# Attention heads with half units in another place, outputs by groups of four heads, and a mixer in another order

## The reference

```python
y = concatenate([o_a, o_b])            # layer 0: 10 sparse heads, 6 dilated heads
x = x + (y * silu(gate)) @ w_out       # layer 1: 8 stick breaking heads, 8 forgetting heads

# the second block
x = x + 0.5 * rmsnorm(swiglu(rmsnorm(x)))            # width 5632
o = gb[0] * o_cmp + gb[1] * o_sel + gb[2] * o_win    # 8 heads, 2 groups of keys and values
h = rglru(conv(xb)) * gelu(yb)                       # 1024 channels, the recurrent part
x = x + rmsnorm(concatenate([rmsnorm(o), rmsnorm(h)]) @ w_out)
x = x + 0.5 * rmsnorm(swiglu(rmsnorm(x)))            # width 5632 again
x = x + rmsnorm((gelu(x @ w_ple_gate) ...) @ w_ple_proj)
```

## Time and profile before

| what | value |
|---|---|
| time, median of 3 runs | 3042.7 us (3040.08 to 3045.18) |
| the profiled execution: time, span | 3044.3 us, 3042.5 us |
| PE busy in the span | 2920.7 us, 96% |
| DVE busy | 1728.0 us, 57% |
| ACT busy | 1298.8 us, 43% |
| POOL busy | 14.2 us |
| DMA | 530.6 MB, 174 GB/s |
| chain of waits that ended last | PE 64%, DVE 4%, ACT 2% |
| layer 0's heads | 280 to 366 us |
| layer 1's last head | 871 us |
| mixer, first unit to w_out's first | 1744 to 2090 us |

### The profile page before, as it was taken

How to read it: one execution, slowest core, us unless ns; L and a number is a source line. 1 busy time by engine, 2 the same in 40 slices (tenths; PEclk the granted TensorE clock), 3 DMA queues, 4 the chain that set the end, 5 groups by cost and what they waited for, 6 DMA issues and landing times.

```text
span 3042.5 us, 33344 instructions
## 1 busy us (share of the span) xinstructions
PE 2920.7 (96%) x13590; PEld 2419.7 (80%) x13590; DVE 1728.0 (57%) x1622; ACT 1298.8 (43%) x1340; POOL 14.2 (0%) x17
## 2 busy tenths in 40 slices
PE   8999899999989999999999999777999999999997
PEld 7878788878878888888888788665788888888876
DVE  5468755445465555555555744764655555555574
ACT  5444444344444433333433545443443333333453
POOL 0000000000000000000000000000000000000000
PEclk9999999999999999999999999997999999999999
DMA  6545255544445555555555554412565555555544
GB/s 237 194 147 183 95 183 180 193 165 165 134 140 186 196 192 193 193 190 188 188 193 192 168 186 166 165 56 97 169 208 193 193 189 188 188 193 191 189 170 141
DMA packets 275615, 530.60 MB, mean 174 GB/s; under 512 B 8640, under 2 KB 30288, under 8 KB 274752
## 3 DMA queue, kind: packets, MB, share of 16 engines
q1 hardware_dynamic: 275088, 528.25, 51.8%
q0 software_dynamic: 432, 0.99, 0.1%
HBM read 527.12 MB, written 2.10 MB: 174 GB/s over the span
## 4 chain that ended last, share of the span: by engine, by line
PE 64%; DVE 4%; ACT 2%; issue 1%; DMA 0%; SPq 0%; DVEq 0%; ACTq 0%
PE ps L594 19%; PE ps L596 19%; PE ps L595 19%; PE ps L612 1%; PE ps L613 1%; PE ps L614 1%; PE ps L674 1%; DVE w_lo L1615 1%; PE ps L760 0%; ACT w_hi L1101 0%; PE ps L1058 0%; PE ps L704 0%; PE ps L780 0%; DVE st L1848 0%; DMA raw<-in_w_in 0%
## 5 line engine op out<-in xcount | busy, mean ns | idle before, releaser
L1615 DVE TENSOR_TENSOR w_lo<-raw,w_hi 128x2048 fp32r<-128x2048 f32 (+2 forms) x503 | 1126.8, 2244 | 833.2 <-ACT w_hi L1101 831.6
L1101 ACT ACTIVATE w_hi<-raw 128x2048 fp32r<-128x2048 f32 (+2 forms) x503 | 942.0, 1878 | 1028.0 <-DMA raw<-in_ff_w_down 320.5
L594 PE MATMUL ps<-w_hi,x_hi 128*128 128x512 f32 (+3 forms) x3176 | 1234.0, 389 | 11.9 <-DVE w_lo L1615 11.9
L596 PE MATMUL ps<-w_hi,x_lo 128*128 128x512 f32 (+3 forms) x3176 | 1225.0, 386 | 0.0
L595 PE MATMUL ps<-w_lo,x_hi 128*128 128x512 f32 (+3 forms) x3176 | 1224.3, 385 | 0.0
L594 PEld LDWEIGHTS ps<-w_hi,x_hi 128*128 128x128 f32 x3176 | 599.3, 189 | 133.6 <-DVE w_lo L1615 11.3
L596 PEld LDWEIGHTS ps<-w_hi,x_lo 128*128 128x128 f32 x3176 | 598.3, 188 | 119.3
L595 PEld LDWEIGHTS ps<-w_lo,x_hi 128*128 128x128 f32 x3176 | 599.3, 189 | 116.1
L594 PE MATMUL ps<-w_hi,h_hi 128*128 128x512 f32 x652 | 254.8, 391 | 2.0 <-DVE h_lo L2331 2.0
L595 PE MATMUL ps<-w_lo,h_hi 128*128 128x512 f32 x652 | 254.5, 390 | 0.0
L596 PE MATMUL ps<-w_hi,h_lo 128*128 128x512 f32 x652 | 254.3, 390 | 0.0
(11 more groups left out here) (290 smaller groups left out, 1542.3 us busy)
## 6 DMA issues: line engine op xcount, KB each, us to landing
raw<-in_w_in SPq DMA_DIRECT2D x143, 1024.0 KB, 5.0
raw<-in_ff_w_gate SPq DMA_DIRECT2D x88, 1024.0 KB, 5.0
raw<-in_ff_w_up SPq DMA_DIRECT2D x88, 1024.0 KB, 5.0
raw<-in_ff_w_down SPq DMA_DIRECT2D x88, 1024.0 KB, 5.1
raw<-in_w_out SPq DMA_DIRECT2D x48, 1024.0 KB, 5.0
raw<-in_w_ple_gate SPq DMA_DIRECT2D x16, 1024.0 KB, 5.1
z<-in_rows SPq DMA_DIRECT2D x5, 1024.0 KB, 7.2
raw<-in_w_in SPq DMA_DIRECT2D x8, 536.0 KB, 3.6
```

The lines of the kernel that those rows point to most:

```text
L594: nc.tensor.matmul(o, x[0][:, k0 + c, s], hi[:, c, 0:width], start=first and c == 0, stop=False)
L596: m = nc.tensor.matmul(o, x[1][:, k0 + c, s], hi[:, c, 0:width], start=False, stop=last and c == n - 1)
L1101: nc.scalar.activation(landed_part(w_hi, u, j), landed_part(raw, u, j), ACT.Copy).then_inc(hi_ready, 1)
L1615: V.tensor_tensor(landed_part(w_lo, u, j), landed_part(raw, u, j), landed_part(w_hi, u, j).bitcast(F32), ALU.subtract).then_inc(parts_read ...
```

## The change

**Layer 0's heads.** On PE the half unit of an iteration moves behind `logits(n+1)`. ACT and DVE keep their orders.

**Outputs by four heads, layers 0 and 1.** The plan interleaves the first two column blocks of w_out unit by unit, so that both take the units of group 0 first, then of group 1, and so on. `gate_heads(layer, g)` for groups 0 and 1 stands in DVE's loop of heads (behind heads 9 and 13, and behind 28 and 30), for 2 and 3 behind it. PE transposes group 0 in front of `mix` of head 10 in layer 0, and between units at head 30 in layer 1, where the first unit of w_out runs beside head 31.

**The mixer.** The compressed part's columns come first, then a block of 352, then five blocks interleaved: 348 columns, `w1` of the keys, 348 columns, `w1` of the values, 512 columns. Queries, window and selected keys follow. Each kind's four heads of a group follow one another: four window, four selected, four window, four selected. The second block of queries and 7 halves and more of w_out (the recurrent part's rows first) run as half units behind `logits(n+1)` of a head. The compressed part becomes two transposes of a padded tile and four 128x512 matmuls, and one addition for four heads. `out_gain` has a buffer of its own; the block with `out_part` is kept in SBUF and added later. The norm of the attention part is summed by groups. SP loads in the new order, with the small weights behind the keys' `w1`; POOL's clearing of the buffer is gone.

```diff
-    L0_OUT = plan(t["w_out0"], 0, [BW] * 4)
+    L0_OUT = out_blocks(t["w_out0"])
...
+    def out_blocks(w):
+        k = [(c, UC) for c in range(0, KC, UC)]
+        first = in_turn([(w, 0, BW, k), (w, BW, BW, k)], [0, 1] * 4)
+        plan(w, 2 * BW, [BW] * 2)
+        return first
...
-    MIX_REC = plan(t["w_in_2"], ZG, [BW] * 3 + [268, 268])
-    MIX_QKV = plan(t["w_in_2"], 0, [BW] * 5)
-    CMP = plan_other(4)
+    MIX_COMPRESSED = plan(t["w_in_2"], ZKC, [BW])
+    MIX_REC = plan(t["w_in_2"], ZG, [352])
+    MIX_TOGETHER = in_turn([...],
+                           [0, 0, 1, 0, 1, 0, 1, 2, 1, 2, 2, 3, 2, 3, 4, 3, 4, 3, 4, 4])
...
+    halves_beside = [2, 2, 1, 1, 1, 1, 0, 0] + [1] * 7 + [0]
...
                         turn_qk(n + 1)
-                    if n < 16:
-                        advance_half(n % 2)
-                    if n > n0:
+                    if n == 46:
+                        turn_compressed()
+                    elif n == 11:
+                        turn_y(0, 0)
+                    if n > n0 and (n < 16 or n >= 32):
                         mix(n - 1)
-                    if n >= 16:
+                    if 16 < n < 32:
+                        mix(n - 1)
+                    if n == 30:
+                        advance(1)
+                        turn_y(1, 0)
+                        advance(2)
+                    elif n == 31:
+                        next_y(1)
+                    elif 16 <= n < 32:
                         advance(beside[n])
                     if n + 1 < n1:
                         logits(n + 1)
+                    if n < 16:
+                        advance_half(n % 2)
+                    elif n >= 32:
+                        advance_halves(n)
+                    if n >= 46:
+                        mix_compressed(n - 46)
                     turn_probs(n)
+                if n1 == 48:
+                    advance_half(1)
+                    mix(47)
+                    return
+                layer = n1 // 16 - 1
+                turn_y(layer, 1)
+                next_y(layer)
                 mix(n1 - 1)
+                next_y(layer)
+                turn_y(layer, 2)
+                next_y(layer)
+                turn_y(layer, 3)
+                while at[0] < first_unit[OUT_OF[layer] + 2]:
+                    next_y(layer)
...
+            def mix_compressed(g):
+                bank = 2 * pair_of[OUT_PART]
+                if g == 0:
+                    pe.wait_ge(made["cmp_p_copied"], 1)
+                else:
+                    pe.wait_ge(made["cmp_added"], g)
+                for tt in range(NT):
+                    i = nc.tensor.matmul(ps[:, bank + tt, :], cmp_pT[:, tt * P:(tt + 1) * P],
+                                         cmp_vs[:, g * BW:(g + 1) * BW], start=True, stop=True)
...
+                    if n in (9, 28):
+                        gate_heads(n // 16, 0)
+                    elif n in (13, 30):
+                        gate_heads(n // 16, 1)
```

More of the change, by code:

```diff
@@ L481, in _ @@
                 load_block(L0_GATE + b)
-            for b in range(4):
-                load_block(L0_OUT + b)
+            load_units(first_unit[L0_OUT], end_unit[L0_OUT + 3])
             sp.wait_ge(group_gated, 4)
@@ L989, in _ @@
                 i.then_inc(made[done], 1)
-                advance(2)
-            advance(4)
-            pe.wait_ge(made["rec_out_squared"], 1)
-            for b in range(LB):
-                i = nc.tensor.matmul(ps[:, 4, 0:SEQ], ones[:], by_block(r2)[:, b, :], start=b == 0, stop=b == LB - 1)
-            i.then_inc(made["rec_summed"], 1)
-            advance(2)
+            until(first_unit[MIX_TOGETHER])
+            pe.wait_ge(st_done, turned_before["mix"] + 8)
             pe.wait_ge(rotated, 3)
-            pe.wait_ge(made["rec_norm_root"], 1)
             for m, c0 in enumerate((ZKC, ZVC)):
@@ L1040, in _ @@
-            i.then_inc(made["cmp_kv_made"], 1)
-            pe.wait_ge(made["cmp_kv_ready"], 1)
+            for k in range(2):
+                i = nc.tensor.matmul(ps[:, 7, P:2 * P], cmp_hidT_heads[:, k, :], cmp_w2[:, 1, k, :],
+                                     start=k == 0, stop=k == 1)
+            i.then_inc(made["cmp_kv_made"], 1)
+            until(first_unit[MIX_SELECTED] + 1)
+            pe.wait_ge(made["rec_out_squared"], 1)
+            for b in range(LB):
+                i = nc.tensor.matmul(ps[:, 4, 0:SEQ], ones[:], by_block(r2)[:, b, :], start=b == 0, stop=b == LB - 1)
@@ L1067, in _ @@
+            for s in range(4):
+                turn_attention(s)
+                if s == 1:
+                    pe.wait_ge(st_done, turned_before["attn"] + 2)
+                    advance(1)
+            pe.wait_ge(st_done, turned_before["attn"] + 4)
+            until(end_unit[MIX_OUT + 3] - 1)
             advance_by_tile(signal=True)
@@ L1138, in drain @@
                     i.then_inc(drained[pair_of[b]], 1)
+                elif kind == "part":
+                    for tt in range(NT):
+                        i = nc.scalar.activation(out_part[:, tt], summed(b)[:, tt], ACT.Copy)
+                    i.then_inc(drained[pair_of[b]], 1)
+                elif kind == "output" and b == MIX_OUT + 2:
+                    act.wait_ge(made["part_added"], 1)
+                    tail_sums([out_part[:, tt] for tt in range(NT)], 2)
                 elif kind == "output":
@@ new lines, in _ @@
+            advance(1)
+            for tt in range(NT):
+                if tt == 0:
+                    act.wait_ge(made["attn_left"], 1)
+                else:
+                    act.wait_ge(out_written, 48)
+                attention_squares(tt, 1, made["attn_squared"])
+                act.wait_ge(made["attn_squared"], 3 + tt)
+                if tt == 0:
+                    act.wait_ge(made["attn_based"], 1)
+                nc.scalar.activation(attn_root[:, tt:tt + 1], attn_ssq[:, tt, 1:2], ACT.Sqrt,
+                                     bias=attn_base[:, tt:tt + 1]).then_inc(made["attn_rooted"], 1)
```

754 lines of the change are left out of this document (476 added, 278 removed).

## The result

The changed kernel took 3023.3 us in the median of 4 runs (3023.0 to 3024.7), the kernel before 3041.8 us in the same session (4 runs, 3040.1 to 3045.2). The ratio is 0.9939 with a 95% interval of 0.9921 to 0.9956. A second session gave 3027.3 us (3023.9 to 3029.4) against 3040.9, ratio 0.9951 (0.9933 to 0.9967). So the change saves 13.5 to 18.5 us, where 34.5 were forecast. The sign held, and both medians lie in the whole range of 2983 to 3032; the second lies outside the 2990 to 3025 that went with the likeliest course. The size was 39 to 54% of the forecast.

What follows compares the result with a forecast made beforehand. PE, busy 96% of the 3042.5 us span, was taken as the bound. Terms +11.5 - 9 - 42 + 5 = -34.5 against 3044.3 gave 3009.8, less 1.6: 3008 us; likeliest range 2990 to 3025, whole range 2983 to 3032.

Steps and rivals of the forecast that it cites:

- Part 1: Layer 0's heads: half unit behind the next logits makes a pair 12.5 us instead of 10.06; 7.5 pairs cost 18.4.
- The walk: Row-by-row timing of the changed heads in layer 0 and the mixer; left no single wait over 1.5 us.
- Part 2: Outputs by four heads: layer 0's tail gains 11.3 us, its gating costs 2.8; layer 1 nets -9 us.
- Part 3: Mixer, from its first products through its heads to w_out: 338.7 us instead of 380.4, so -42.
- +5 for the clock: Mixer: two long waits of 6.4 us each cost some 2 to 3 us more through slow matmuls behind them.
- (a): Layer 0's heads: the late half unit is free because splits land where DVE is idle; 2986 us, chance 0.12.
- (b): Mixer's heads: rounds longer by 1.3 us each, 20 in all, from ACT's split before an exponential; 3028 us, chance 0.12.
- (c): Two-head rounds of layer 0 and mixer: clock falls, slower kernel; 65 us if three in four matmuls slow, 3073; chance 0.08.
- (d): Layer 0: both copies of a pair queue behind a split, about 30 us more; 3038 to 3042, chance 0.06.

Runs made afterwards that it cites:

- e1: Changed kernel with layer 0's half unit put back ahead of mix(n-1): 3001.7 us.
- e2: Kernel before with one part of the change alone, layer 0's half unit behind the next logits: 3064.5 us.
- e9: Changed kernel with ACT's rounding ahead of the exponentials in every second head of layer 0, half units still behind the logits: 3017.5 us.
- e5: Changed kernel with DVE splitting the compressed rows ahead of a narrow unit and ACT's two small operations one unit later: 3017.2 us.
- e6: Changed kernel where, behind the mixer's heads, the recurrent unit of w_out no longer waits for the attention part's first split: 3012.0 us.
- e4: Changed kernel with the two pairs of PSUM banks swapped from the second block of queries on: 3022.2 us.
- e11: Changed kernel run once more, unaltered: 3027.3 us.
- e8: Changed kernel with the edits of e1, e3, e4, e5, e6 and e7 together: 2961.6 us, ratio to before 0.9739.
- e3: Changed kernel with the half units beside the mixer's heads put ahead of mix(n-1): 3010.8 us.
- e7: Changed kernel with the first two column blocks of w_out0 and w_out1 interleaved to end two units apart, not one: 3022.7 us.
- e10: e8 with ACT's rounding ahead of the exponentials in every second head of layer 0: 2960.6 us, ratio to before 0.9736.

## Why the prediction was right, and where it was off

**Part 1 held in its numbers.** 12.54 us a pair against 12.5 forecast, L780's line 24.4 us later against 22.7 (the gating took 4.2 and not 2.8), layer 0's net +11.9 against +11.5. e1 and e2 show the cause from both sides: it is the place of the half unit. The walk had the new lengths of both heads of a pair (5.8 and 6.7), so the pair is no luck; its account of what made them longer was too simple: the split in front of the copy is a third of the 2.48 us (e9), and the first head, called no dearer, became 1.2 us longer without one.

**Part 2 held where it was priced.** The tail of layer 0 gave 12.5 us (11.3 forecast). In layer 1, what PE loses between 866 and 950 us fell from about 14 to 5, the 9 us of the forecast (an estimate: the stretch less the products in it, at their usual spacing of 0.23 us for 512 columns, 0.12 for 260 and 0.11 for 128). What failed is the step's end: I had followed the gain up to w_out and not to the next norm. There 3 us were given back, as the wait of 2.49 us at 994 instead of 1.43, with a slow clock behind it, so that the net is -5.8.

**Part 3 is the term that was mis-sized.** Forecast -42 and +5 for the clock, -37; measured -29.2 from the mixer's first product to the last unit of w_out. Its waits were right: 6.4 forecast and 6.58 found for the first compression unit, 6.4 and 6.59 behind the heads, 2.6 and 2.33 for the second pair, 98.1 and 100.7 us for the heads. Ahead of the heads it took 219.4 us against 214.0, from L1130 and from the slow products behind its wait. The clock's +5 was the step that failed: I let each long wait cost 2 to 3 us. From the mean clocks of three of the rows above, 0.98 over 220 us, 0.97 over 101 and 0.79 over 32, the engine was at the low level for some 9, 6 and 13 us, which costs half of that where it was at work: 10 to 14 us, an estimate. e5 and e6 bear it out: with a wait of 5.7 us removed 9.7 went, with 8.5 removed 13.4.

**What the prediction left out** is the second SwiGLU's start, +2.3 us. The change adds a block to the plan, so the parity of the PSUM pairs turned, and a product that uses a fixed pair has to wait for the last drain (e4). And +0.9 in the mixer's first block, whose cause was not tried.

**The rivals.** (a), layer 0 free: refuted by e1 and e2. (b), longer rounds in the mixer: 2.6 us longer in all, not 20. (c), the clock in the two-head rounds: the mechanism exists (e11), at some 3 us, not 65, since it came behind few of these waits. The walk that spoke against it was wrong in one point: it had no wait over 1.5 us in these rounds, and changed shows 2.42 to 2.53 us in three rounds of layer 0 and 2.62 and 2.65 in the mixer's heads. (d) fell: one copy of a pair waits, not both. Its price did not follow from Part 1 either: a second copy behind a split would have added 2.45 us to each of 7.5 pairs, 18 and not 30. The misses add up to the 13.6 us between the forecast's 34.5 and the 20.9 of the two spans, to rounding: 7.8 in the mixer, 3.2 in layer 1, 0.4 in layer 0, 2.3 and 0.9 at places left out, and 1.0 the other way at the end.

**Could more be had?** Yes: the kernel with the parts of e8 takes 2961 us, 2.6% less than before, four to six times what the change alone gives. One of the three things that the change does, the half unit behind the logits, is a loss in both places where it stands.

## What to carry to other kernels

Filler work belongs ahead of the instruction that waits, not behind it: the same 12 products cover a copy and a negation when they stand in front of them, and cover nothing when they follow. Price a long wait of PE at its length and some 60 to 70% more for the clock behind it, as e5 and e6 measured on waits of 2.3 to 6.6 us, and follow a gain to the next place where all engines meet before it is booked. When a plan gets a block more or less, look at everything that uses a fixed buffer, since the alternation turns.

## What the runs showed of the hardware

The granted clock fell behind waits that I had thought harmless, and not each time. In eight profiles the wait ahead of the first SwiGLU is 2.47 to 2.49 us: in seven of them the clock was 0.79 over the next 8 us, in e3 it was 1.00. In the three with 2.23 or 2.24 us there (e7, e8, e10) it was 1.00. In the kernel before, a wait of 2.64 us at 1975.5 us left it at 1.00 over 1974 to 1984 us, so the prediction's "behind waits of 2.61 us and more" does not hold for each of them. In layer 0's heads, waits of 1.3 to 2.5 us with work between them gave 0.89 to 1.00 in different executions of the same instructions. So a wait costs more than its length by an amount that differs from one execution to the next, and the place where it differs is seen in the timeline: layer 0's last head starts its transposes between 388.4 and 392.6 us in the seven profiles with such waits, and between 368.0 and 368.5 in the three with the half unit first. The whole time does not show it as clearly: the changed kernel's two medians lie 4 us apart, those of e8 and e10 1 us, but the four runs of e10 spread over 6 us.
